# Two to four output tiles made together, the pieces of the operand in the outer loop

## The reference

```python
proj = x @ w_in[i]                                   # queries, keys, values, latents, gates
q_mla = _rms_norm(q_lat, q_norm_g[i]) @ w_uq[i]      # q_lat, kv_lat: the latents
...
ple = jax.nn.sigmoid(x @ w_ple_gate[i]) * (p[i] @ w_ple[i])      # embedding gates
x = _layer_norm(DEEPNORM_ALPHA * x + f + ple, ln2_g[i], ln2_b[i])
...
logits = x @ w_router + b_router                     # layer 1: top 2 of 8 experts
...
h = rms_norm(x, g_mix) @ w_in_2                      # second block; first columns: queries
...
h2 = rms_norm(x, g_ffn)                              # last feed-forward
return x + (jax.nn.silu(h2 @ w_gate) * (h2 @ w_up)) @ w_down
```

## Time and profile before

| | us |
|---|---|
| median of 3 runs | 2127.78 (2125.83 to 2128.56) |
| the profiled execution, its own time | 2127.19 |
| its span in the profile | 2125.4 |
| PE busy | 2068.4, 97% of the span |
| DVE busy | 1445.6, 68% |
| ACT busy | 960.2, 45% |
| mean granted clock of TensorE | 0.988 of full |

### The profile page before, as it was taken

How to read it: one execution, slowest core, us unless ns; L and a number is a source line. 1 busy time by engine, 2 the same in 40 slices (tenths; PEclk the granted TensorE clock), 3 DMA queues, 4 the chain that set the end, 5 groups by cost and what they waited for, 6 DMA issues and landing times.

```text
span 2125.4 us, 27888 instructions
## 1 busy us (share of the span) xinstructions
PE 2068.4 (97%) x11194; PEld 1758.6 (83%) x11194; DVE 1445.6 (68%) x1471; ACT 960.2 (45%) x1006; POOL 77.8 (4%) x43
## 2 busy tenths in 40 slices
PE   8999999999999989999999999999999989989998
PEld 8877789988877878888888888888888868668998
DVE  4332577774333578888888888898888953346765
ACT  0133110001133267777778787777877733331000
POOL 1001200000001110000000000000000000100000
PEclk9999999999999999999999999999999999999999
DMA  9632479753613459999999999999999973324520
GB/s 349 231 130 101 144 254 335 255 166 107 237 65 119 159 205 373 373 389 386 379 382 380 379 382 381 367 389 377 383 381 392 385 275 124 119 80 161 197 100 21
DMA packets 171754, 553.25 MB, mean 260 GB/s; under 512 B 9248, under 2 KB 89760, under 8 KB 128272
## 3 DMA queue, kind: packets, MB, share of 16 engines
q1 hardware_dynamic: 162832, 517.55, 65.7%
q10 hardware_dynamic: 6912, 25.02, 2.9%
q0 software_dynamic: 1920, 9.40, 1.2%
HBM read 528.09 MB, written 23.59 MB: 260 GB/s over the span
## 4 chain that ended last, share of the span: by engine, by line
PE 96%; DVE 2%; ACT 1%; issue 1%; DMA 0%; DVEq 0%; SPq 0%; ACTq 0%
PE act_ps L1060 29%; PE dve_ps L1085 14%; PE act_ps L836 12%; PE dve_ps L952 9%; PE act_ps L952 7%; PE dve_ps L836 7%; PE job_ps L1021 3%; PE job_ps L1013 3%; PE act_ps L980 2%; PE job_ps L899 1%; PE job_ps L1068 1%; PE job_ps L918 1%; PE act_ps L1184 1%; PE job_ps L930 1%; PE dve_ps L1388 1%; PE job_ps L1388 1%
## 5 line engine op out<-in xcount | busy, mean ns | idle before, releaser
L2100 DVE TENSOR_TENSOR weights_rest<-weight_ring,expert_short 128x2048 fp32r<-128x2048 f32 x336 | 762.6, 2289 | 106.0 <-ACT expert_short L1560 105.7
L1560 ACT ACTIVATE expert_short<-weight_ring 128x2048 fp32r<-128x2048 f32 x336 | 640.6, 1917 | 101.0 <-PE act_ps L1060 68.3
L1060 PE MATMUL act_ps<-expert_short,tokens_short 128*128 128x512 f32 x896 | 355.2, 396 | 5.4 <-DVE tokens_rest L2110 5.4
L1060 PE MATMUL act_ps<-expert_short,tokens_rest 128*128 128x512 f32 x896 | 350.1, 391 | 0.0
L1060 PE MATMUL act_ps<-weights_rest,tokens_short 128*128 128x512 f32 x896 | 350.1, 391 | 0.0
L1461 ACT ACTIVATE arena_mla<-act_ps 128x256 f32<-128x256 f32 (+1 forms) x72 | 31.1, 432 | 406.8 <-PE act_ps L952 307.3
L1060 PEld LDWEIGHTS act_ps<-expert_short,tokens_short 128*128 128x128 f32 x896 | 169.0, 189 | 39.6 <-DVE weights_rest L2100 5.7
L1060 PEld LDWEIGHTS act_ps<-expert_short,tokens_rest 128*128 128x128 f32 x896 | 168.8, 188 | 36.5
L1060 PEld LDWEIGHTS act_ps<-weights_rest,tokens_short 128*128 128x128 f32 x896 | 169.2, 189 | 33.8
L2029 DVE TENSOR_TENSOR weights_rest<-weight_ring,ffn_weights_short 128x2048 fp32r<-128x2048 f32 x66 | 151.3, 2292 | 2.3
L1085 PE MATMUL dve_ps<-expert_short,hidden_short 128*128 128x512 f32 x448 | 139.5, 393 | 0.0
(11 more groups left out here) (350 smaller groups left out, 3437.0 us busy)
## 6 DMA issues: line engine op xcount, KB each, us to landing
weight_ring<-in_moe_w SPq DMA_DIRECT2D x336, 1024.0 KB, 7.0
weight_ring<-in_w_in SPq DMA_DIRECT2D x44, 1024.0 KB, 7.4
weight_ring<-in_ffn_w SPq DMA_DIRECT2D x32, 1024.0 KB, 7.2
weight_ring<-in_w_out SPq DMA_DIRECT2D x12, 1024.0 KB, 6.4
weight_ring<-in_w_gate SPq DMA_DIRECT2D x11, 1024.0 KB, 5.2
weight_ring<-in_w_up SPq DMA_DIRECT2D x11, 1024.0 KB, 7.8
weight_ring<-in_w_down SPq DMA_DIRECT2D x10, 1024.0 KB, 7.0
weight_ring<-in_w_ple_gate SPq DMA_DIRECT2D x8, 1024.0 KB, 6.1
```

What stands on the lines that cost most here:

```text
L1060: m = nc.tensor.matmul(bank[0:CAP, :], a[:, 4 * c + k, :], w[:, k, :], start=(c == k == i == 0), stop=(c == 1 and k == 3 and i == 2))
L1560: nc.scalar.activation(shorts[u % SHORTS][:, :], ring[:, slot, half], ACT.Copy).then_inc(moe_w_short, 1)
L2100: V.tensor_tensor(ring_lo[slot][:, half], ring[:, slot, half], shorts[u % SHORTS][:, :], ALU.subtract)\
```

## The change

It makes several tiles together where their operand comes piece by piece. In `first_pair` the four tiles of the last feed-forward's first two units share one loop over the pieces; in `ple_rows` the two token tiles do; the first two latents of layer 1, and the last queries with the key tile, do as well. The number of matmuls and their operands stay the same, and the programs of DVE, ACT, POOL and SP aren't touched. `places` now follows all of unit 4.

```diff
-                    for r, bank in enumerate(banks):
-                        for k in range(4):
-                            if i < 6 and r == 0:
-                                pe.wait_ge(*after(4 * c + k))
+                    for k in range(4):
+                        if i < 6:
+                            pe.wait_ge(*after(4 * c + k))
+                        for r, bank in enumerate(banks):
                             for p, (a, w) in enumerate(((0, short), (1, short), (0, rest))):
                                 m = nc.tensor.matmul(bank[:, :], ff_x[a][:, 4 * c + k, r * P:(r + 1) * P], w[:, k, :],
                                                      start=(c == k == p == 0), stop=(c == 1 and k == 3 and p == 2))
-                        if c:
-                            m.then_inc(act_tile_ready, 1)
-                        if beside and i == 4 and r == 0:
-                            beside()
+                            if c and k == 3:
+                                m.then_inc(act_tile_ready, 1)
                     if c == 0:
                         m.then_inc(ple_unit_used, 1)
+                    if beside and i == 4:
+                        beside()
...
+            def first_pair(units, after):
+
+                pe.wait_ge(ffn_w_split, n.unit + 2)
+                parts = [(tiles(ff_w[u][:, :], DT), tiles(ring_lo[units[u][1] % SLOTS][:, u * 2048:(u + 1) * 2048], DT)) for u in range(2)]
+                banks = [[act_bank(), act_bank()], [dve_bank(), dve_bank()]]
+                for k in range(DT):
+                    pe.wait_ge(*after(k))
+                    for u, (short, rest) in enumerate(parts):
+                        for j in range(2):
+                            for i, (a, x_part) in enumerate(((short, 0), (short, 1), (rest, 0))):
+                                m = nc.tensor.matmul(banks[u][j][:, 0:SEQ], a[:, k, j * P:(j + 1) * P], ff_x[x_part][:, k, :],
+                                                     start=(k == i == 0), stop=(k == DT - 1 and i == 2))
+                            if k == DT - 1:
+                                m.then_inc(dve_tile_ready if u else act_tile_ready, 1)
...
+                    if l and i == 0:
+                        banks, after = [dve_bank(), dve_bank()], normed_x(2 * l)
+                        for k in range(DT):
+                            pe.wait_ge(*after(k))
+                            for j, bank in enumerate(banks):
+                                m = nc.tensor.matmul(bank[:, 0:SEQ], w[:, k, j * P:(j + 1) * P], xs[k], start=k == 0, stop=k == DT - 1)
+                                if k == DT - 1:
+                                    m.then_inc(dve_tile_ready, 1)
+                        w = w[:, :, 2 * P:]
...
-            two_tiles(dve_bank(), in2(0, "qa"), dve_tile_ready, lambda k: (rms_ready, k + 1))
-            product(dve_bank()[:, 0:SEQ], two_columns(0, "ksa"), zs).then_inc(dve_tile_ready, 1)
+            qa_bank, kk_bank, qa_w, kk_w = dve_bank(), dve_bank(), in2(0, "qa"), two_columns(0, "ksa")
+            for k in range(DT):
+                pe.wait_ge(rms_ready, k + 1)
+                for j in range(2):
+                    m = nc.tensor.matmul(qa_bank[:, j * SEQ:(j + 1) * SEQ], qa_w[k][:, j * P:(j + 1) * P], zs[k], start=k == j == 0,
+                                         stop=k == DT - 1, skip_group_check=True)
+                    if k == DT - 1 and j:
+                        m.then_inc(dve_tile_ready, 1)
+                m = nc.tensor.matmul(kk_bank[:, 0:SEQ], kk_w[k], zs[k], start=k == 0, stop=k == DT - 1)
+            m.then_inc(dve_tile_ready, 1)
```

10 lines of the change are left out of this document (7 added, 3 removed).

## The result

| | before | after |
|---|---|---|
| median of 6 runs, us | 2127.72 (2125.83 to 2128.61) | 2136.57 (2129.07 to 2137.54) |
| span of the profiled execution | 2125.4 | 2134.9 |
| PE busy | 2068.4 | 2068.6 |
| mean granted clock | 0.988 | 0.986 |

The ratio is 1.0038, with an interval of 1.0027 to 1.0048: slower, and by more than the bound of 0.2%. The forecast was 2132.8, range 2130.0 to 2136.0, or +5.0 us over the 2127.78 of before; the medians differ by 8.8 us. The direction is right, and the size is about 1.8 times what I said. Five of the six runs lie between 2136.37 and 2137.54; the sixth took 2129.07 at a granted clock of 0.990.

The account below looks back on a forecast made before the run. TensorE bounds the kernel, 96% of the chain, so its waits and clock count. Terms 2.25 + 2.05 + 0.5 + 0.3 + 0.2 = +5.3 us gave 2132.5 to 2133.1, stated as 2132.8 us, range 2130.0 to 2136.0.

Parts of the forecast that it names:

- the prefix sums: Router sums in layer 1's gates: 2.7 us later, hidden by 0.9 us; 0 taken, up to +1 if scatters land later.
- Gates of layer 1: Before the experts: the first bank is read 2.05 us later, so PE starts the experts later; +2.05 us, bounds 0 and 2.7.
- Last feed-forward: Third unit waits for its weight split, starting 0.55 us later, then a second clock fall costs 1.7: +2.25 us.
- Rival 1: Feed-forward and experts: both stalls come but the clock forgives them; sum +2.6 to +3.6 us, chance 0.25.
- The rule on dense work: Last feed-forward: by the skill's advice on contiguous work both clock falls are absent, about -0.95 us; 0.05 of the 0.25.
- Last queries: Last queries with the key tile: PE waits for ACT's squares, no piece was waited for; +0.5 us.
- latents: Layer 1's latents: the third tile waits for DVE's copy of the first; +0.3 us, bounds 0 and +0.4.
- gates of layer 0: Layer 0's embedding gates: transposes behind the last unit wait for the first bank's read; +0.2 us, bounds 0 and 0.5.
- Rival 3: Last feed-forward: the third unit's split isn't waited for, -2.55 in place of +2.25 us, sum +0.5; chance 0.06.

Follow-up runs that it names:

- places_late: The kernel before with only the router's prefix sums moved behind all of unit 4 of layer 1's embedding gates: 2130.24 us, ratio 1.0013.
- after_held: The changed kernel, with SP asking for the sixth block of the first expert's weights only when the four scatters have landed: 2126.55 us, ratio 1.0003.
- after_held_load: The changed kernel, with the sixth block of the first expert's weights asked for only when the first rows have landed: 2128.18 us, ratio 1.0006.
- gates_mid: The kernel before with the embedding gates' token tiles together in both layers, the prefix sums still behind twelve matmuls of unit 4: 2125.86 us, ratio 0.9997.
- ff_four: The kernel before with only the four tiles of the last feed-forward's first two units sharing the loop over the pieces: 2128.56 us, ratio 1.0013.
- after_places_mid: The changed kernel with the prefix sums put back behind twelve matmuls of unit 4: 2127.71 us, ratio 1.0006.
- latents_queries: The kernel before with only the change's parts at the latents of layer 1 and the last queries: 2126.98 us, ratio 0.9999.
- places_first: The kernel before with the prefix sums moved ahead of unit 4 of the embedding gates: 2124.64 us, ratio 0.9991.
- best2: The kernel before with the last feed-forward's first unit's two tiles together and the prefix sums ahead of unit 4: 2122.29 us, ratio 0.9976.
- ff_four_third: The kernel before with the last feed-forward's four tiles together and a third buffer for the third unit's short part: 2125.76 us, ratio 0.9997.
- ff_two: The kernel before with only the two tiles of the last feed-forward's first unit together, the second unit behind them: 2124.49 us, ratio 0.9988.

## Why the prediction was right in direction and wrong in size

**What failed: the prefix sums.** The step was "Hidden by 0.9 us; 0 taken, up to +1 if the scatters land later". The first half held: the sums, and POOL's first scatter, came 3.2 us later. But I moved the load of the rows by the delay of the sums, and gave scatters and load the time that they took before. SP's queue was not put beside POOL's: its next weights, 2 MB at 759, were 0.7 us behind the fourth scatter and are now ahead of two of them, and the 2 MB at 771 are ahead of the load. Three of the scatters took 10.3 to 10.6 us where the four had taken 3.4 to 7.0, the load took 7.3 for 4.5, and 0.9 us of cover became a wait of 8.7. `places_late` shows that the position of the sums alone does it (+5.8 at this place); `after_held` and `after_held_load` that the weights in flight are the cause, since the same late scatters and the same load are fast once these are held. The trace of before had the warning: its fourth scatter, the one nearest to SP's block, already took 7.0 us. The bound of +1 should have been drawn from that and from the DMA share of the stretches. Of after, from 760 to 770 in steps of 2 us:

```profile
760.00:762.00 2.00, 2.00 (x10) 1.61 (x10) 1.97 (x2) 0.00 (x0) 1.70 (x2) 1.00 0.98 170
762.00:764.00 2.00, 2.00 (x11) 1.65 (x10) 1.97 (x4) 0.00 (x0) 1.57 (x1) 1.00 1.00 416
764.00:766.00 2.00, 2.00 (x10) 1.68 (x9) 1.86 (x7) 0.00 (x0) 0.00 (x0) 1.00 1.04 428
766.00:768.00 2.00, 2.00 (x10) 1.66 (x9) 0.53 (x5) 0.00 (x0) 0.00 (x0) 1.00 1.01 403
768.00:770.00 2.00, 2.00 (x11) 1.65 (x10) 0.00 (x0) 0.00 (x0) 0.00 (x0) 1.00 0.97 395
```

The last two columns are the DMA engines' share and GB/s: full for 10 us. The trace of before is nearly as full from 758 to 768 (0.86 to 1.02); there two of the scatters have landed when SP's block begins at 758.54, and the third lands at 760.0. The Trainium skill, "DMA: Bandwidth & Descriptors", Queues, rings and completion order, says that each DMA engine takes turns between the queues that have work for it, a packet at a time; the trace agrees in so far as each transfer that shared the time with a block of weights slowed down, whichever was issued first: the last three scatters, 4.3 to 5.5 us in `after_held`, are 10.3 to 10.6 in after, and the load takes 3.5 us alone and 7.3 behind a block. How the packets took turns, no run here shows.

**Gates of layer 1, +2.05.** The mechanism is right: the wait for `tokens_rest` grows to 7.5 us in `gates_mid` and in `after_held_load`. The experts' first matmul moves by 2.03 and 2.04 us there, as the sum had it; net it is 0.9 us, about my lower bound, as the low stretch forgives 1.1. In the changed kernel itself this term is buried under the rows, and the clock gives back 1.2 us there, since PE starts so late that most of the low stretch falls into its wait.

**Last feed-forward, +2.25.** Right in its sum and in each step: +2.24 in after, +2.23 in `ff_four`. Its second half is luck in part. Five traces have the four tiles and the wait of 3.0 us; in these two the clock falls behind it, in `after_places_mid`, `after_held` and `after_held_load` it doesn't. Of the last:

```profile
1938.40:1941.60 3.20, 0.79 (x6) 0.79 (x7) 3.13 (x5) 0.36 (x2) 0.00 (x0) 1.00 0.77 256
1941.70:1945.10 3.40, 3.40 (x30) 3.40 (x30) 3.33 (x4) 0.38 (x1) 0.00 (x0) 1.00 0.92 371
```

The wait of 3.00 us stands in the first stretch, and there and in the second the clock is 1.00; the place costs 0.76 us there, and 0.75 in each of the other two, near the 0.55 that the wait alone was to cost. Rival 1 is thus real. What decides it the runs don't show; the wait is the same, and only its time in the program is another.

**The rule on dense work**, by which both falls would be absent (-0.95). After shows both, and in all thirteen traces the first fall comes. What denser work does here is to end it sooner: in the five kernels with the old order of the first unit (before, `latents_queries`, `places_late`, `gates_mid`, `places_first`) the low stretch behind the restart is 6.8 or 6.9 us long, in the eight that make two or four tiles together it is 3.4. The advice of the Trainium skill, "TensorE: Matmul & The Clock Gate", HAM oscillation — how this bites in real kernels, to work contiguously over K before the next wait so that PE stays warm, is thus borne out in part: the fall isn't avoided, but the low stretch is half as long.

**Last queries +0.5, latents +0.3, gates of layer 0 +0.2.** Measured +0.58, +0.46, +0.17: the latents are just above my upper bound of 0.4, the others as the steps had them.

**Rival 3**, the split not waited for, wanted -2.55. With the third buffer it gained 1.45: I had overlooked that the four tiles also hold both of ACT's banks until its table is loaded, for which PE waits 0.83 us.

**The sum.** With 5.7 for 2.05 at the experts it is +9.0 for the 9.5 of the trace; most of the other 0.5 are the clock and the start, in places that the change doesn't touch. I had named rows that come late as what would make the prediction wrong, and gave it no price and no place in the range. It is also what made the direction come out. With the rows on time the same change, in `after_places_mid` and `after_held_load`, measures 1.0006 (0.9997 to 1.0015), which is not slower by the bound: the second fall at the feed-forward is absent there, and the low stretches between 1840 and 1900 are fewer. Slower for the reasons that I had summed is thus not shown for the whole kernel, only place by place; the direction was luck in part.

## What to carry to other kernels

A delayed instruction can cost more than its delay when it issues transfers: look which queue's transfers it will now share its time with, also those issued just behind it, and whether the DMA engines' share is already full where it lands. Then go on down the lists of the engines that wait: here a second wait of PE came 20 us behind the first. When several tiles share the loop over the pieces, everything that lay beside the later tiles (splitting the next weights, reading the banks, a table load) loses its cover; two tiles gained all there was, four turned the gain into a wait. Where a chain ends in a small transfer that many wait for, hold back the large prefetch that nobody waits for yet.

## What the runs showed of the hardware that was not expected

The clock's low stretches come and go with shifts of a few us, in places where the work is unchanged. The kernel before, from 1874.7, and the same times in `after_held_load` (PE's work there is shifted by 1.2 us at the first stretch and by 0.4 at the last):

```profile
1874.70:1878.00 3.30, 3.30 (x12) 1.17 (x12) 2.16 (x12) 2.93 (x11) 0.00 (x0) 0.50 0.00 0
1878.20:1888.20 10.00, 7.98 (x47) 5.16 (x44) 3.24 (x12) 3.81 (x14) 0.00 (x0) 1.00 0.00 0
1888.40:1891.80 3.40, 3.40 (x9) 2.75 (x9) 1.09 (x7) 0.35 (x1) 0.00 (x0) 0.50 0.00 0
```

```profile
1874.70:1878.00 3.30, 2.58 (x18) 1.49 (x20) 1.18 (x8) 2.49 (x12) 0.00 (x0) 1.00 0.00 1
1878.20:1888.20 10.00, 7.43 (x44) 4.71 (x40) 3.34 (x14) 3.82 (x10) 0.00 (x0) 1.00 0.00 0
1888.40:1891.80 3.40, 3.09 (x14) 2.71 (x15) 1.88 (x10) 1.18 (x6) 0.00 (x0) 1.00 0.00 0
```

Between 1840 and 1900 the table above has -3.7 to -3.9 us for `latents_queries`, `places_late`, both `after_held` kernels and `after_places_mid`, -3.1 for `gates_mid`, `places_first` and `best2`, and nothing for after, `ff_four`, `ff_four_third` and `ff_two`. Over a whole execution the low time was from 34.1 to 54.6 us. So of the 8.1 us between the ends of the traces of `after_held` and after, 3.3 are at the experts (+2.4 for +5.7), 3.9 between 1840 and 1900 and 1.5 at the feed-forward are clock, less 0.6 elsewhere. Single runs of one kernel differ in the same way: the sixth run of after is 7.3 us or more below its other five, at a clock of 0.990 for 0.986 or 0.987. What decides whether a given idle stretch is followed by a fall stays open: the runs show it only by its effect. A difference of under some 4 us in one trace of this kernel is not a step's cost unless it stands at the step's place.
